# A two-block transformer on one core: the first block's mixer with an exponential in place of the sigmoid, query roots applied at the maxima, one filter tap on ScalarE, and one value unit cut in two

## The reference, cut to what matters

```
h = rms_norm(x) ; z = h @ w_in                # 2824 columns
6 full causal heads:        q,k = rms_norm(rope(..)); softmax(q k^T / 8) v
6 windowed heads, 2 keys:   the same with a window of 128 and a sink per head
4 mLSTM heads:              q,k = silu(causal_conv(z, 4 taps) + b)
                            h = (q k^T * decay) v / max(|den|, exp(-m))
                            y = rms_norm(h * sigmoid(o)) * gain
x = x + concat(heads) @ w_out
x = x + relu(rms_norm(x) @ w_up)^2 @ w_down   # width 4096
```

## Time and profile before

| what | value |
|---|---|
| median of 3 runs | 1688.56 us (1687.88 to 1688.7) |
| the profiled execution: its own time, its span | 1688.8 us, 1687.0 us |
| TensorE busy | 1663.8 us |
| VectorE, ScalarE, GpSimd busy | 1231.7, 988.6, 197.5 us |
| granted clock of TensorE | 1.00 |
| first mixer, second mixer | from about 13 to 137 us, and the same sequence some 296.8 us later |

### The profile page before, as it was taken

How to read it: one execution, slowest core, us unless ns; L and a number is a source line. 1 busy time by engine, 2 the same in 40 slices (tenths; PEclk the granted TensorE clock), 3 DMA queues, 4 the chain that set the end, 5 groups by cost and what they waited for, 6 DMA issues and landing times.

```text
span 1687.0 us, 25619 instructions
## 1 busy us (share of the span) xinstructions
PE 1663.8 (99%) x9966; PEld 1450.2 (86%) x9966; DVE 1231.7 (73%) x1977; ACT 988.6 (59%) x1656; POOL 197.5 (12%) x170
## 2 busy tenths in 40 slices
PE   6999999999999999999999999999999999999999
PEld 5788888877888888888888988888888888998888
DVE  7777765767776568876677877767886677778774
ACT  5676654567665455554577665545555467765542
POOL 2621000152200000000521000000000242100000
PEclk9999999999999999999999999999999999999999
DMA  7625555542655655556533555555555643345553
GB/s 283 200 101 190 198 195 200 206 161 101 237 191 196 212 178 197 188 206 228 206 122 127 195 178 200 189 201 188 196 187 200 257 163 128 143 174 199 198 200 125
DMA packets 62022, 313.98 MB, mean 186 GB/s; under 512 B 22685, under 2 KB 24353, under 8 KB 25294
## 3 DMA queue, kind: packets, MB, share of 16 engines
q1 hardware_dynamic: 60382, 303.93, 50.4%
q0 software_dynamic: 1232, 4.22, 0.9%
q10 hardware_dynamic: 288, 4.19, 0.7%
HBM read 311.25 MB, written 7.36 MB: 189 GB/s over the span
## 4 chain that ended last, share of the span: by engine, by line
PE 92%; ACT 4%; DVE 3%; issue 1%; DMA 0%; SPq 0%; DVEq 0%; ACTq 0%
PE acc L415 46%; PE acc L417 23%; PE acc L404 4%; PE acc L405 4%; PE acc L406 4%; DVE w_lo L390 2%; ACT w_hi L381 1%; PE acc L424 1%; PE acc L426 1%; PE acc L425 1%; PE tp L828 1%; PE tp L812 1%; ACT work L861 1%; PE sc L801 1%; PE acc L571 0%
## 5 line engine op out<-in xcount | busy, mean ns | idle before, releaser
L390 DVE TENSOR_TENSOR w_lo<-raw,w_hi 128x1024 fp32r<-128x1024 f32 (+1 forms) x564 | 678.5, 1210 | 295.8 <-ACT w_hi L381 294.1
L381 ACT ACTIVATE w_hi<-raw 128x1024 fp32r<-128x1024 f32 (+1 forms) x564 | 583.0, 1038 | 187.7 <-PE acc L417 120.2
L415 PE MATMUL acc<-act_a,w_hi 128*128 128x512 f32 x1440 | 506.1, 395 | 1.2 <-DVE w_lo L390 1.2
L415 PE MATMUL acc<-hidden,w_hi 128*128 128x512 f32 x1216 | 421.8, 392 | 0.0
L417 PE MATMUL acc<-act_a,w_lo 128*128 128x256 f32 x1440 | 402.4, 279 | 0.0
L417 PE MATMUL acc<-hidden,w_lo 128*128 128x256 f32 x1216 | 339.7, 279 | 0.0
L415 PEld LDWEIGHTS acc<-act_a,w_hi 128*128 128x128 f32 x1440 | 269.6, 187 | 64.6 <-issue 5.3
L417 PEld LDWEIGHTS acc<-act_a,w_lo 128*128 128x128 f32 x1440 | 271.8, 189 | 0.1
L415 PEld LDWEIGHTS acc<-hidden,w_hi 128*128 128x128 f32 x1216 | 227.5, 187 | 50.5
L589 ACT COPY part<-acc 128x256 f32<-128x256 f32 x272 | 101.2, 372 | 281.3 <-PE acc L417 280.2
L415 PE MATMUL acc<-act_b,w_hi 128*128 128x512 f32 x688 | 239.4, 392 | 0.0
(11 more groups left out here) (228 smaller groups left out, 2064.3 us busy)
## 6 DMA issues: line engine op xcount, KB each, us to landing
raw<-in_slabs SPq DMA_DIRECT2D x282, 1024.0 KB, 4.8
na_skew<-in_rpb SPq DMA_DIRECT2D x32, 128.0 KB
na_bias<-na_skew ACTq DMA_DIRECT2D x2, 2048.0 KB, 8.1
t_skew<-t_by_distance POOLq DMA_DIRECT2D x2, 1024.0 KB, 14.6
t_bias<-t_skew POOLq DMA_DIRECT2D x1, 2048.0 KB, 10.5
x_res<-in_x SPq DMA_DIRECT2D x1, 1024.0 KB, 5.0
out_x<-x_res SPq DMA_DIRECT2D x8, 128.0 KB, 4.6
prow<-in_prow SPq DMA_DIRECT2D x1, 518.0 KB
```

What stands on the lines that cost most here:

```text
L381: nc.scalar.activation(w_hi[u % RING][:, 0:n], raw[j % RAW][:, (u % 2) * HALF:(u % 2) * HALF + n], ACT.Copy).then_inc(s["unit_hi"], 1)
L390: nc.vector.tensor_tensor(w_lo[u % RING][:, 0:n], raw[j % RAW][:, (u % 2) * HALF:(u % 2) * HALF + n], w_hi[u % RING][:, 0:n].bitcast(F32), ...
L415: nc.tensor.matmul(bank[:, :], wh, src[:, c + i, :, :].rearrange("p i s -> p (i s)"), start=first and i == 0, stop=False, skip_group_check ...
```

## The change

Five edits, all in the mixer of the first block:

- The output gate: ScalarE writes exp(-o) in place of sigmoid(o); GpSimd adds one to it (128x512); VectorE takes the reciprocal (128x512, in place) as the first instruction of `y_first`.
- Queries are no longer multiplied by their roots. `normalise` and its GpSimd twin cover the keys alone. The root of the query row goes into `first` as the factor on the scores (a per-partition operand in place of the constant 1.0).
- The first of the four taps, with its bias, is two ScalarE activations out of PSUM ahead of each copy of the convolution's input. VectorE does the other three.
- Value unit 1 is issued as two halves, with `scores(4)` between them. `scores(6)` keeps its place.
- In VectorE's order in the group before, `mean_squares(1)` and `lstm_probs(0)`, `lstm_probs(1)` stand ahead of `rope_a(1)`.

```diff
-            for i in range(n):
+            for i in range(n) if part is None else (part,):
...
-        SCORES_AT = {0: (4, 6), 4: (10,), 6: (12,), 8: (14,)}
+        SCORES_AT = {0: (6,), 4: (10,), 6: (12,), 8: (14,)}
...
+        def keys_and_roots(k):
+            h0, h1 = QK_HEADS[k]
+            first = TYPES1[k][1][0]
+            r = rstd_h[:, R1_AT[k]:R1_AT[k + 1]].rearrange("p (t h) -> p t h", t=T)[:, :, first:]
+            return (by_head(qk[:, :, (h0 + first) * HD:h1 * HD]),
+                    r.unsqueeze(3).broadcast_to([P, T, h1 - h0 - first, HD]))
+        def query_root(n, t):
+            k, n = (0, n) if n < MOBA else (1, n - MOBA)
+            at = R1_AT[k] + t * (QK_HEADS[k][1] - QK_HEADS[k][0]) + n
+            return rstd_h[:, at:at + 1]
...
-                    value_columns(1)
+                    value_columns(1, (0,))
+                    scores(LSTM)
+                    value_columns(1, (1,))
                     turn_tiles(f["heads", 2], qk, 4 * P)
...
+                for c in (2 * i, 2 * i + 1):
+                    ins = nc.scalar.activation(cv1[:, c, :], tp[bank][:, c % 2 * S:(c % 2 + 1) * S], ACT.Identity,
+                                               bias=pcol1[:, l, C_CONVB + c:C_CONVB + c + 1],
+                                               scale=pcol1[:, l, C_CONV + c * TAPS + TAPS - 1:C_CONV + (c + 1) * TAPS])
+                ins.then_inc(s["conv_done"], 1)
                 nc.scalar.copy(xT[:, 2 * i:2 * i + 2, :], tp[bank][:, :].rearrange("p (c s) -> p c s", s=S))\
...
-            nc.scalar.activation(zxo, zxo, ACT.Sigmoid).then_inc(s["xo_ready"], 1)
+            nc.scalar.activation(zxo, zxo, ACT.Exp, scale=-1.0).then_inc(s["xo_ready"], 1)
...
-                for k in range(TAPS):
+                for k in range(1, TAPS):
+                    wait(dve, value(b, "conv_done", i * TAPS + k))
...
+                if i == LSTM + MOBA:
+                    wait(dve, value(b, "qrs_ready", 2))
...
-                                                         hd["mask"][:, HALVES1[t]], 1.0, start, ALU.add, ALU.min,
+                                                         hd["mask"][:, HALVES1[t]], query_root(hd["n"], t), start,
+                                                         ALU.add, ALU.min,
...
             def y_first():
+                wait(dve, value(b, "xo_one", 1))
+                nc.vector.reciprocal(zxo, zxo)
                 wait(dve, value(b, "floor_ready", 1))
...
                     normalise(0)
+                    mean_squares(1)
                     dve_split(dve, b, b.unit - n + RING + 2)
+                    lstm_probs(0)
+                    lstm_probs(1)
                     wait(dve, value(b, "sink_ready", 1))
                     rope_a(1)
-                    lstm_probs(0)
-                    lstm_probs(1)
-                    mean_squares(1)
...
+            to, r = keys_and_roots(1)
+            nc.gpsimd.tensor_tensor(to, to, r, ALU.mult).then_inc(s["qk_ready"], 1)
+            zxo = z1[:, :, ZXO:ZXO + LSTM * HD]
+            wait(pool, value(b, "xo_ready", 1))
+            nc.gpsimd.tensor_scalar(zxo, zxo, 1.0, None, ALU.add).then_inc(s["xo_one"], 1)
...
             wait(pool, value(b, "lstm_seen", 1))
-            wait(pool, value(b, "xo_ready", 1))
```

More of the change, by code:

```diff
@@ L330, in build @@
             qsq_ready qms_ready qrs_ready tables_ready rope_a_ready rope_b_ready rope_sum qk_ready normed
-            conv_seen gates_seen gate_abs gate_ln gate_rows gcol_ready floor_ready conv_done silu_conv xo_ready
+            conv_seen gates_seen gate_abs gate_ln gate_rows gcol_ready floor_ready conv_done silu_conv xo_ready xo_one
             heads_t sink_ready score_seen d_seen w_ready lstm_prob exp_done prob_ready probT_ready pair_hi pair_lo
@@ L344, in build @@
                       rope_b_ready=2, rope_sum=2, qk_ready=2, conv_seen=2, gates_seen=1, gate_abs=1, gate_ln=1,
-                      gate_rows=1, gcol_ready=1, floor_ready=1, conv_done=2 * TAPS, silu_conv=1, xo_ready=1, heads_t=5,
+                      gate_rows=1, gcol_ready=1, floor_ready=1, conv_done=2 * TAPS, silu_conv=1, xo_ready=1, xo_one=1, heads_t=5,
                       sink_ready=1, score_seen=MOBA + SWA, d_seen=LSTM, w_ready=LSTM, lstm_prob=LSTM,
@@ L392, in dve_split, with columns_unit @@
                 b.made += 1
-        def columns_unit(u, src, c, banks, w, first, last):
+        def columns_unit(u, src, c, banks, w, first, last, part=None):
             n = len(PLAN[u][1])
-            for i in range(n):
+            for i in range(n) if part is None else (part,):
                 for t in range(T):
@@ L1026, in pe_layer1, with value_columns @@
             o_before = [b.fill(("acc", i), (s["x_new"], x0 + 1 + k))[1] for k, i in enumerate(v_banks)]
-            def value_columns(n):
+            def value_columns(n, parts=(0, 1)):
                 if n == 0:
@@ L1031, in value_columns @@
                         wait(pe, before)
-                u = pe_unit_in(pe, b)
-                columns_unit(u, act_a, 2 * n, [acc[i] for i in v_banks], GROUP, n == 0, n == DC // 2 - 1)\
-                    .then_inc(s["units_used"], 1)
+                for k in parts:
+                    if k == 0:
+                        pe_unit_in(pe, b)
+                    mm = columns_unit(b.unit - 1, act_a, 2 * n, [acc[i] for i in v_banks], GROUP, n == 0,
+                                      n == DC // 2 - 1, k)
+                if k:
+                    mm.then_inc(s["units_used"], 1)
             pair0 = b.at("pair") - (MOBA + SWA) // 2
@@ L1314, in taps @@
                 wait(dve, value(b, "conv_seen", i + 1))
-                for k in range(TAPS):
+                for k in range(1, TAPS):
+                    wait(dve, value(b, "conv_done", i * TAPS + k))
                     for c in (2 * i, 2 * i + 1):
                         wcol = pcol1[:, l, C_CONV + c * TAPS + TAPS - 1 - k:C_CONV + c * TAPS + TAPS - k]
[L1318 to L1325, removed]
+                        ins = nc.vector.scalar_tensor_tensor(out=cv1[:, c, k:S], in0=xT[:, c, 0:S - k], scalar=wcol,
+                                                             in1=cv1[:, c, k:S], op0=ALU.mult, op1=ALU.add)
                     ins.then_inc(s["conv_done"], 1)
@@ L1354, in normalise @@
             def normalise(k):
-                h0, h1 = QK_HEADS[k]
-                m0, m1 = R1_AT[k], R1_AT[k + 1]
-                to = by_head(qk[:, :, h0 * HD:h1 * HD])
                 wait(dve, value(b, "rope_sum", k + 1))
                 wait(dve, value(b, "qrs_ready", k + 1))
-                r = rstd_h[:, m0:m1].rearrange("p (t h) -> p t h", t=T)
-                nc.vector.tensor_tensor(to, to, r.unsqueeze(3).broadcast_to([P, T, h1 - h0, HD]), ALU.mult)\
-                    .then_inc(s["qk_ready"], 1)
+                to, r = keys_and_roots(k)
+                nc.vector.tensor_tensor(to, to, r, ALU.mult).then_inc(s["qk_ready"], 1)
             def lstm_probs(m):
@@ L1623, in pool_layer1 @@
             wait(pool, value(b, "qrs_ready", 2))
-            r = rstd_h[:, R1_AT[1]:R1_AT[2]].rearrange("p (t h) -> p t h", t=T)
-            nc.gpsimd.tensor_tensor(by_head(to), by_head(to), r.unsqueeze(3).broadcast_to([P, T, h1 - h0, HD]), ALU.mult)\
-                .then_inc(s["qk_ready"], 1)
+            to, r = keys_and_roots(1)
+            nc.gpsimd.tensor_tensor(to, to, r, ALU.mult).then_inc(s["qk_ready"], 1)
+            zxo = z1[:, :, ZXO:ZXO + LSTM * HD]
+            wait(pool, value(b, "xo_ready", 1))
+            nc.gpsimd.tensor_scalar(zxo, zxo, 1.0, None, ALU.add).then_inc(s["xo_one"], 1)
             wait(pool, value(b, "lstm_seen", 1))
-            wait(pool, value(b, "xo_ready", 1))
             for t in range(T):
```

## The result

The changed kernel takes 1696.4 us (median of 4 runs, 1696.02 to 1697.97) against 1688.63 us before; the ratio is 1.0051, with a 95% interval of 1.0039 to 1.0062. The forecast was 1695.7 with a range of 1692.0 to 1700.5. The profiled execution took 1696.51 us, with a span of 1694.7.

The account below looks back on a forecast made before the run. TensorE, busy 1663.8 of 1687.0 us, was taken as the bound. With R, the reciprocal, at 4.1 us, a layer loses R - 0.56 = 3.54; two layers' 7.1 on 1688.6 give 1695.7 us, range 1692.0 to 1700.5.

Parts of the forecast that it names:

- the delay behind the reciprocal: VectorE's reciprocal ahead of first(12) makes head 12's exponentials start at 100.68 + R in place of 101.24 us.
- The likeliest case: Reciprocal delays head 12's exponentials, without a fall of TensorE's clock: 1695.7 us, own range 1692.3 to 1696.7, chance 0.74.
- matmuls at half rate around 106 us: Sign in the changed profile that would make the forecast wrong: TensorE at about half speed near 106 us.
- the clock: Rival: TensorE falls to its lower clock in the new stall, 4.3 us more over both layers, 1700.0 us; chance 0.12.
- The term R: Time of the 128x512 reciprocal on VectorE at the head of y_first: 4.1 us, bounds 2.4 and 4.6.
- R - 0.56: Loss of one layer in us, R being the reciprocal's time: 3.54 with R = 4.1.
- The three new waits: TensorE waits on VectorE's divisions at turn(8) and turn(9), and on maxima ahead of scores(14): 4 us together.
- The halves: Value unit 1 split around scores(4): maxima wait gone, scores(6) 0.7 us earlier, then waiting about 0.7 for heads 2's copy.
- The table loads: Two ScalarE loads of 1.28 us go: the gate's worth nothing, the one before head 4's exponentials makes turn(4) 0.44 us earlier.
- Costed at nothing: GpSimd's add is hidden, roots in the maxima cost 0.06 us an instruction (0.24 a pair), tap on ScalarE costs nothing.
- The streaming rival: VectorE's reciprocal takes only 0.69 us, a layer loses 0.13, and the time is 1688.9 us; chance 0.12.
- The all-gain rival: All three TensorE waits go and the reciprocal is hidden: 4.9 us off, 1683.7 us; chance 0.02.

Follow-up runs that it names:

- e8: The changed kernel with reciprocals and multiplications of 8 to 512 elements a partition added behind VectorE's last work; ran once, 1702.64 us.
- e3: The changed kernel with extra matmuls on constants filling TensorE's three new waits, their result unread; 1694.07 us, ratio 1.0033 to the kernel before.
- e4: The changed kernel with only the gate edit undone: sigmoid kept on ScalarE, no add, no reciprocal; 1693.56 us, ratio 1.0028 to the kernel before.
- e10: The kernel before with a tanh gate, the value unit in halves and heads 2 turned ahead of scores(4), nothing else; 1685.25 us, ratio 0.9981.
- e7: The changed kernel with a tanh gate, no reciprocal, and heads 2 turned between the first half unit and scores(4); 1685.48 us, ratio 0.9983.
- e5: The kernel before with the gate edit alone: exponential, GpSimd's add, and the reciprocal at the head of y_first; 1695.58 us, ratio 1.0044.
- e6: The kernel before with the gate as 0.5 + 0.5 tanh(o/2) and nothing else; 1688.26 us, ratio 1.0000.

## Why the prediction came out

The sign, the place and the delay behind the reciprocal were right. The likeliest case as a whole was not: the forecast named matmuls at half rate around 106 us as a sign that it is wrong, and there they are, from 105.7 to 109.1. That the point came within 0.7 us of the median is luck: the reciprocal was put 1.5 us too high over two layers, and the clock, worth 2.3, was left out.

*The reciprocal was sized too high.* The term R was 4.1 us with bounds of 2.4 and 4.6; it is 3.35, also below the 3.5 to 4.6 that the forecast wanted to see. That takes 0.75 off a layer. The flatter of the two slopes in the earlier trace rows, 6.5 ns an element, was the right one. The two groups of four elements differ by 9 ns, and this alone put 1.1 us between the two values whose middle I took. The lower bound was no better: the add's 13 ns for four elements are no measure of fixed cost. The Trainium skill's repeat count of 8 (VectorE: DVE Perf Modes, section "Walkthrough: the 8-slice pipeline in each mode"), read as eight steps, made an estimate of 4.3 us. The chip takes 6.24 ns an element (e8), and the measurement decides.

*The clock was put with the rivals, at 0.12, and it happened.* Each layer had 3.4 us at half rate, worth 1.2 us by e3, where the rival's price was 2.15. What I held against it, that 1.38 us of idle time at 84.09 left no mark, says nothing of a stall with 2.08 busy microseconds in 5.30. So the likeliest case, the reciprocal's delay without a fall of the clock, did not happen: with the true R it makes 2.79 a layer and 1694.2, which is what e3 measured, 1694.07. With the clock's 2.3 it is 1696.5, against a measured 1696.4.

*The delay behind the reciprocal* was right as a formula. R - 0.56 gives 2.79, and the exponentials of head 12 came 2.72 later. The three new waits stand where the forecast put them (`turn(8)`, `turn(9)`, `scores(14)`), 3.2 us together in place of 4, in line with the shorter reciprocal.

*The halves.* The wait on the maxima went and the copy of heads 2 took its place with 0.68 us, as forecast. The gain was 0.48 us (84.09 to 83.18, less 0.43) in place of 0.7; the 0.22 between them is what the two halves take longer than the whole unit, which the sum had at nothing.

*The table loads.* `turn(4)` is 0.34 us earlier (92.42 to 91.65, less 0.43) in place of 0.44, so the 0.14 us that the halves had gained more were indeed lost in its longer wait, 0.77. That the load at the gate's line was worth nothing fits. e4 shows the other at 1.4 us: `turn(4)` waits 2.18 with it and 0.77 without.

*Costed at nothing.* GpSimd's add took 1.49 us at 79.06 and was over 14 us before VectorE wanted it. The pointer costs 0.06 us an instruction as assumed: groups by shape of the changed kernel against the earlier trace rows,

```profile
L1404 DVE CUSTOM_DVE_ANT_0 work<-sc,mask_s,neg_sink 128x128 f32<-128x128 f32 x8 | 3.2, 404 | 4.0 <-PE sc L955 4.0
L1404 DVE CUSTOM_DVE_ANT_0 work<-sc,mask_m,rstd_h 128x128 f32<-128x128 f32 x8 | 2.8, 348 | 8.3 <-PE sc L955 8.3
```

348 against 289 ns, and 404 against 350. The tap's two activations took 1.02 us together, and ScalarE still waited 0.28 for the gates. e10 confirms roots and tap as worth nothing.

*The streaming rival* is refuted by e8. *The all-gain rival* had nothing for it in the change, but e7 and e10 show how much of its 4.9 us could be had with another order: 3 us.

## What to carry to other kernels

Price an operation by its slope over sizes, not by its name, and before you swap a function on one engine for an operation on another, look at what queues behind it there: the same reciprocal cost 8 us in front of a maximum, the clock's 2.3 among them, and nothing that can be measured in two gaps of the same engine. When a wait is taken away, ask what was late behind it; here one move of the turn brought 2 us, and all else of the change, without its reciprocal, 0.7 at most. A stall of TensorE can cost more than its length, and its surcharge can be measured by filling it.

## What the runs showed of the hardware that I had not expected

- With a single wait of 2.18 us in each mixer the mean clock was under 1.000 in four executions of six, with times some 2.6 us apart (e4, place of the spells not traced). With the longer, broken stall it was under 1.000 in every execution of the change (three waits, 3.21 us together, 2.08 us busy in 5.30) and of e5 (2.72 us together). With 1.38 us of waiting at most it was 1.000 in every run of before. The spell at the lower level can be twice as long: in the profiled execution of e8 the granted clock was 0.50 from about 102.5 to 109.3 us. The changed kernel's one run of 1697.97 us has a mean clock of 0.997 where the other three have 0.998.
- At the start of the kernel the granted clock reads 1.00 while matmuls of 264 columns start 0.22 us apart; later they start 0.12 us apart. The slow pace is that of the spell in the changed kernel, where matmuls of 256 columns start 0.21 us apart at a granted clock of 0.50, so it is the lower level. How soon this ends differs between executions by up to 1.4 us in the start of the first mLSTM scores (68.53 in e5, 69.91 in e7), and this is more than the worth of a whole edit. e6 and e7 can be told apart by their medians over eleven runs, not by one execution of each.
- Four divisions by a pointer on VectorE (`seconds(8)`) take 2.81 us before and 2.78 after the change, both times while GpSimd does its gate multiplications, and 1.01 us where GpSimd is idle (at 86.83 us in the changed kernel). So this delay is no part of the loss, though it lies in front of `first(12)` in both.
